# Modulation vectors as plain float32 matmuls on four column groups, spread over the layer; the latent-attention rotation folded into the score product

## The reference, cut to what matters

```python
mod = jax.nn.silu(c) @ w_ada[l] + b_ada[l]          # c for latents, c_ctx for the prompt
shift1, scale1, gate1, shift2, scale2, gate2 = jnp.split(mod, 6, axis=-1)
h = rms_norm(x, norm1) * (1 + scale1) + shift1
x = x + gate1 * mixing(h)            # differential, latent (MLA) and windowed attention
h = rms_norm(x, norm2) * (1 + scale2) + shift2
x = x + gate2 * expert_choice_ffn(h) # 16 experts, top-k per expert
```

## Time and profile before

| | us |
|---|---|
| median of 3 runs | 3476.33 (3473.27 to 3481.16) |
| the profiled execution | 3475.3, span 3473.5, mean TensorE clock 0.953 |
| TensorE busy (matmuls) | 3142.9 (90%) |
| VectorE busy | 2289.6 (66%) |
| ScalarE busy | 1699.7 (49%) |
| modulation stage, first matmul to first value product, layer 0 / layer 1 | 89.85 / 90.36 |

### The profile page before, as it was taken

One profiled execution on the slowest core, in us unless ns is written; L12 is line 12 of the kernel. 1 busy time (PEld: TensorE's weight loads), 2 busy tenths in 40 slices (PEclk: granted clock), 3 DMA queues, 4 the chain that ended last, 5 costly groups with the idle time before them and its releaser, 6 DMA issues.

```text
span 3473.5 us, 44790 instructions
## 1 busy us (share of the span) xinstructions
PE 3142.9 (90%) x15742; PEld 2212.6 (64%) x15742; DVE 2289.6 (66%) x3210; ACT 1699.7 (49%) x2471; POOL 0.2 (0%) x4
## 2 busy tenths in 40 slices
PE   6988998999978999999889889889899699999994
PEld 2466765667646777777636567557676477777773
DVE  6446535566548888888772654456653688888884
ACT  4425133224126777777573523331420477777773
POOL 0000000000000000000000000000000000000000
PEclk9999999999989999999899999999999799999996
DMA  8410110020217888888781001000112298888881
GB/s 298 178 55 1 60 50 1 26 87 1 103 49 257 303 296 315 314 306 314 243 316 63 31 33 52 26 25 26 63 37 91 89 322 308 308 315 313 314 313 45
DMA packets 276469, 551.00 MB, mean 159 GB/s; under 512 B 13608, under 2 KB 19424, under 8 KB 275680
## 3 DMA queue, kind: packets, MB, share of 16 engines
q1 hardware_dynamic: 273024, 543.32, 43.9%
q10 hardware_dynamic: 3296, 5.67, 0.5%
HBM read 537.52 MB, written 11.44 MB: 158 GB/s over the span
## 4 chain that ended last, share of the span: by engine, by line
PE 77%; DVE 9%; ACT 7%; issue 3%; DVEq 2%; ACTq 2%; DMA 0%; SPq 0%
PE mm L1281 26%; PE mm L791 14%; PE mm L749 11%; PE mm L793 4%; PE mm L853 3%; DVE w_lo L1814 2%; PE mm L821 2%; PE mm L1247 2%; PE mm L1029 2%; PE oo L1260 2%; PE oo L1049 1%; ACT scratch L1356 1%; ACTq L1750 1%; DVE tmp L1814 1%; PE mm L919 1%
## 5 line engine op out<-in xcount | busy, mean ns | idle before, releaser
L1814 DVE TENSOR_TENSOR w_lo<-ring,w_hi 128x1024 fp32r<-128x1024 f32 x864 | 1029.2, 1222 | 102.4 <-ACT w_hi L1356 82.6
L1356 ACT ACTIVATE w_hi<-ring 128x1024 fp32r<-128x1024 f32 x864 | 909.5, 1060 | 302.2 <-PE mm L1281 258.3
L1356 ACT ACTIVATE dw_hi<-ring 128x512 fp32r<-128x512 f32 (+1 forms) x168 | 104.4, 627 | 618.3 <-PE mm L793 612.9
L1814 DVE TENSOR_TENSOR dw_lo<-ring,dw_hi 128x512 fp32r<-128x512 f32 (+1 forms) x168 | 114.9, 689 | 366.1 <-ACT dw_hi L1356 365.6
L791 PE MATMUL mm<-h_hi,dw_lo 128*128 128x512 f32 (+1 forms) x672 | 327.0, 487 | 15.7 <-DVE dw_lo L1814 9.6
L793 PEld LDWEIGHTS mm<-h,ring 128*128 128x128 f32 (+1 forms) x1344 | 256.2, 191 | 61.2
L791 PE MATMUL mm<-h_hi,dw_hi 128*128 128x512 f32 (+1 forms) x672 | 269.5, 401 | 0.0
L791 PE MATMUL mm<-h_lo,dw_hi 128*128 128x512 f32 (+1 forms) x672 | 267.7, 398 | 0.0
L749 PE MATMUL mm<-scratch,ring 128*128 128x512 f32 (+3 forms) x896 | 260.2, 443 | 1.6 <-ACT scratch L1356 1.6
L793 PE MATMUL mm<-h,ring 128*128 128x128 f32 (+1 forms) x1344 | 260.5, 276 | 0.0
L749 PEld LDWEIGHTS mm<-scratch,ring 128*128 128x128 f32 (+1 forms) x896 | 141.3, 191 | 115.3 <-issue 112.9
(11 more groups left out here) (259 smaller groups left out, 5067.7 us busy)
## 6 DMA issues: line engine op xcount, KB each, us to landing
ring<-in_w_ff SPq DMA_DIRECT2D x384, 1024.0 KB, 6.0
ring<-in_w_ada SPq DMA_DIRECT2D x48, 1024.0 KB, 5.5
ring<-in_w_gate SPq DMA_DIRECT2D x24, 1024.0 KB, 6.6
ring<-in_w_in SPq DMA_DIRECT2D x16, 1024.0 KB, 10.0
ring<-in_w_o SPq DMA_DIRECT2D x8, 1024.0 KB, 7.5
x_spill<-x SPq DMA_DIRECT2D x2, 2560.0 KB, 10.6
ring<-in_w_br_da SPq DMA_DIRECT2D x4, 1024.0 KB, 6.8
ring<-in_w_br_mla SPq DMA_DIRECT2D x4, 1024.0 KB, 6.2
```

The source lines that it names most:

```text
L1356: return act.activation(out, in_, ACT.Copy, scale=scale)
L1814: return dve.tensor_tensor(out, in0, in1, op)
```

## The change

**Modulation.** The products are plain float32, without the hi/lo split. A block of 512 columns is 8 matmuls: the k-th 128 channels' part of the vector (2 columns, padded with zeros to 32) against ring tile k; tiles 0 to 3 write to PSUM rows 0, 32, 64 and 96 (four column groups of the array), tiles 4 to 7 add to them. ScalarE copies all 128 rows out, and small matmuls with a 0/1 matrix `fold` sum the four groups and turn the row to columns.

**Where it stands.** Blocks 0 to 3 (shift1, scale1) are first in layer 0; blocks 4 to 6 stand behind the differential attention, 7 to 9 behind the MLA heads, 10 and 11 behind the transposes of `h` in the router, and there in layer 0 also layer 1's blocks 0 to 3. So layer 1 begins with its norm at once. The spill of `x` is issued by ScalarE as soon as `x` is ready.

**MLA.** The query product has 128 output rows: 64, the 32 rotary ones, and the 32 swapped ones, whose weights GpSimd writes into the ring slot. VectorE takes them out of PSUM with two instructions, the second multiplying with a table of cos and sin (`turn32`); the key's rotary rows are there twice, so the score over 128 rows sums both parts. ScalarE now copies all transposed probabilities, ahead of the exponent.

The diff, cut to its core:

```diff
+ADA_BLOCKS = {"ada_first": range(4), "ada_x": range(4, 7), "ada_y": range(7, 10), "ada_z": range(10, 12)}
...
     for b in (2, 0, 1):
         block("in", b * BR)
+    modulation("ada_x")
     gates(0, "br_da")
     block("in", MLA_AT, QR + KVR + MROPE)
     block("in", SWQ_AT)
     out.append(("qb", 0, 0, MH * MQ))
     out.append(("kvb", 0, 0, MH * (MNOPE + MV)))
+    modulation("ada_y")
     gates(1, "br_mla")
     block("in", SWK_AT, 2 * SW_KV * DH)
     gates(2, "br_swa")
     for b in range(2):
         block("o", b * 512)
+    modulation("ada_z")
     return out
     FIRST.setdefault(_c[0], _i)
...
+    ("ada_first", 4), ("norm1", 1), ("da_v", TT), ("da_q", 4), ("da_k_rot", 12), ("da_s", 2), ("ada_x", 3),
     ("da_out", 16), ("mla_in", 10), ("kr_rot", 1), ("mla_v", KEY_TILES),
-    ("mla_heads", MLA_N + 3 * MH), ("mla_out", 16), ("sw_kv_rot", 7),
-    ("sw_s", 2), ("sw_out", 16), ("o", 8), ("norm2", 1), ("router", 1), ("gather_p", 2),
+    ("mla_heads", MLA_N + 2 * MH), ("ada_y", 3), ("mla_out", 16), ("sw_kv_rot", 7),
+    ("sw_s", 2), ("sw_out", 16), ("o", 8), ("norm2", 1), ("router", 1), ("ada_z", 2), ("ada_next", 4), ("gather_p", 2),
     ("pairs", 0)])
...
+                if kind in ADA_BLOCKS:
+                    return a["w_ada"][l, r0:r0 + HALF * P, c0:c0 + width].rearrange("(k p) c -> p k c", p=P)
...
+                def load_first(of, base):
+                    for n in range(FIRST_CHUNKS):
+                        g = base + n
+                        b, k0 = divmod(n, 2)
+                        sp.wait_ge(chunks_free, g + 1)
+                        sp.dma_start(ring[g % RING][:, :, :], chunk_source(of, "ada_first", k0 * HALF, b * 512, 512))\
+                            .then_inc(slot_in[g % RING], 16)
...
+                if l < DEPTH - 1:
+                    load_first(l + 1, PAIR_BASE[l] - FIRST_CHUNKS)
...
-                for n in range(24):
-                    pool.wait_ge(w_ready, ada_part(l, n * UNITS + UNITS - 1))
-                    pool.sem_inc(chunks_free, 1)
+                if l == 0:
+                    for b in range(4):
+                        consumed(MM["ada_first"] + b, 2)
                 consumed(MM["da_v"] + TT - 1, 2)
                 consumed(MM["da_q"] + 3, 2)
                 consumed(DA_K[3], 2)
+                for b in range(3):
+                    consumed(MM["ada_x"] + b, 2)
                 consumed(MM["da_out"] + 7, 3)
                 consumed(MM["da_out"] + 15, 3)
                 consumed(MM["mla_in"] + 3, 2)
                 consumed(SW_Q[3], 2)
+                pool.wait_ge(slot_in[slot(l, FIRST["qb"])], 16 * chunk_use(l, FIRST["qb"]))
+                pool.wait_ge(qb_in, l * 16 + 16)
+                w_ = ring[slot(l, FIRST["qb"])][:, :, :].rearrange("p k c -> p (k c)").rearrange("p (n c) -> p n c", c=P)
+                rot = w_[:, :, MNOPE:MQ].rearrange("p n (i two) -> p n i two", two=2)
+                swapped = w_[:, :, MQ:P].rearrange("p n (i two) -> p n i two", two=2)
+                pool.tensor_scalar(swapped[:, :, :, 0], rot[:, :, :, 1], -1.0, None, ALU.mult)
+                pool.tensor_copy(swapped[:, :, :, 1], rot[:, :, :, 0]).then_inc(wq_ready, 1)
                 consumed(mla_prep(MH - 1, 2), 2)
+                for b in range(3):
+                    consumed(MM["ada_y"] + b, 2)
...
+            def modulate(l, turn, base):
+
+                wait_mm_empty(pe, l, turn)
+                for half in range(2):
+                    g = base + half
+                    pe.wait_ge(slot_in[g % RING], 16 * (g // RING + 1))
+                    for kk in range(HALF):
+                        last = pe.matmul(mm[turn % 2][32 * kk:32 * kk + 32, 0:512], c_cols[:, half * HALF + kk, :],
+                                         ring[g % RING][:, kk, :], start=(half == 0), stop=(half == 1))
+                last.then_inc(mm_full[turn % 2], 1)
+
+            def fold_blocks(l, j, last_turn, blocks):
+
+                wait_mm_read(pe, l, last_turn)
+                if len(blocks) > 1:
+                    wait_mm_read(pe, l, last_turn - 1)
+                wait_t_empty(pe, l, j)
+                for n, row in enumerate(blocks):
+                    for m in range(4):
+                        last = pe.matmul(tp[:, 8 * n + 2 * m:8 * n + 2 * m + 2], row[:, m * P:(m + 1) * P], fold[:, :],
+                                         start=True, stop=True)
+                last.then_inc(t_full, 1)
...
+                if l == 0:
+                    pe.wait_ge(silu_ready, 1)
+                    for b in range(4):
+                        modulate(l, MM["ada_first"] + b, 2 * b)
+                    fold_blocks(l, TR["ada"], MM["ada_first"] + 3, [ada_row[1][:, b, :] for b in range(4)])
+                norm_of_x(l, MM["norm1"], l * 2 + 1)
...
+                for b in range(3):
+                    modulate(l, MM["ada_x"] + b, CHUNK_BASE[l] + FIRST["ada_x"] + 2 * b)
+                fold_blocks(l, TR["ada_x"], MM["ada_x"] + 2, [ada_row[0][:, b, :] for b in range(3)])
...
                     if piece == 0:
-                        product(mm[j % 2][0:MQ, :], lambda k: wqb[:, k, hd * MQ:(hd + 1) * MQ],
-                                lambda k: cq[:, k, :], 2).then_inc(mm_full[j % 2], 1)
-                    elif piece == 1:
+                        product(mm[j % 2], lambda k: wqb[:, k, hd, :], lambda k: cq[:, k, :], 2)\
+                            .then_inc(mm_full[j % 2], 1)
+                    else:
                         for lo, hi in ((0, 512), (512, KEYS)):
                             last = pe.matmul(mm[j % 2][0:MNOPE, lo:hi], wkvb[:, hd, 0:MNOPE], ckv[:, lo:hi],
                                              start=True, stop=True)
                         last.then_inc(mm_full[j % 2], 1)
-                    else:
-                        pe.sem_inc(pe_waited, 1)
-                        pe.matmul(mm[j % 2][MNOPE:MQ, 0:NLAT], c_("swap32", slice(MNOPE, MQ)),
-                                  ml_q[hd % 2][MNOPE:MQ, 0:NLAT], start=True, stop=True).then_inc(mm_full[j % 2], 1)
                 pe.wait_ge(kr_ready, l + 1)
                 pe.transpose(tp[:, 0:P], ckv[:, T:KEYS], ident)
                 pe.transpose(tp[:, P:P + MROPE], ml_k[0][MNOPE:MQ, T:KEYS],
                              ident[MNOPE:MQ, MNOPE:MQ]).then_inc(t_full, 1)
...
+                for b in range(3):
+                    modulate(l, MM["ada_y"] + b, CHUNK_BASE[l] + FIRST["ada_y"] + 2 * b)
+                fold_blocks(l, TR["ada_y"], MM["ada_y"] + 2, [ada_row[0][:, b, :] for b in range(3)])
...
+                z_blocks = 2 if l == DEPTH - 1 else 6
+                for b in range(z_blocks):
+                    modulate(l, MM["ada_z"] + b, CHUNK_BASE[l] + FIRST["ada_z"] + 2 * b)
+                fold_blocks(l, TR["ada_z"], MM["ada_z"] + z_blocks - 1, [ada_row[1][:, b, :] for b in range(z_blocks)])
...
+                def rows_in(turn, row):
+                    wait_mm_full(act, l, turn)
+                    copy(row, mm[turn % 2][:, 0:512]).then_inc(mm_empty[turn % 2], 1)
+
+                act.wait_ge(x_ready, l * 2 + 1)
+                act.dma_start(a["x_spill"], x[:, :, :]).then_inc(x_spilled, 16)
+                squares_of_x(l, 0, 0, lambda k: None)
+                if l == 0:
+                    for b in range(4):
+                        rows_in(MM["ada_first"] + b, ada_row[1][:, b, :])
+                first_rstd(l, 0)
                 shifts(l, 0, 0)
...
                 for s in range(MLA_N + 2):
+                    if s >= 2:
+                        mla_copy(s - 2)
                     if s < MLA_N:
                         hd, t = divmod(s, TT)
-                        if 1 <= t <= 2 and hd < MH - 1:
-                            head_in(hd + 1, t - 1)
+                        if t == 2 and hd < MH - 1:
+                            keys_in(hd + 1)
                         mla_exp(s)
-                    if s >= 2 and s % 2 == 0:
-                        mla_copy(s - 2)
                 wait_o_full(act, l, OO["mla"] + MLA_U - 1)
                 hi_of_tile(l, H_AT["mla_gate"])
+                for b in range(3):
+                    rows_in(MM["ada_y"] + b, ada_row[0][:, b, :])
                 gates(l, MM["mla_out"], lambda: None, H_AT["mla_gate"])
...
+                for b in range(2 if l == DEPTH - 1 else 6):
+                    rows_in(MM["ada_z"] + b, ada_row[1][:, b, :])
...
+                def modulation_in(j, at, n, bias):
+                    wait_t_full(dve, l, j)
+                    return tt(mod[:, at:at + n, :], tp[:, 0:2 * n].rearrange("p (m g) -> p m g", g=2),
+                              bias.unsqueeze(2).to_broadcast([P, n, 2]), ALU.add)
+
+                def gains(n, name):
                     lo, hi = ROWS[name]
                     for g in range(2):
                         stt(gain[:, n, :, g], mod[:, 24 * n + 8:24 * n + 16, g], 1.0, cols[:, lo:hi],
                             ALU.add, ALU.mult)
+
+                b0 = ROWS["b_ada"][0]
```

(32 more changed lines are left out.)

304 lines of the change are left out of this document (128 added, 176 removed).

## The result

| | before | after |
|---|---|---|
| median | 3478.74 us (4 runs, 3473.27 to 3481.27) | 3394.39 us (4 runs, 3392.12 to 3397.75) |
| ratio | | 0.976, 95% interval 0.9743 to 0.9777 |
| span of the profiled execution | 3473.5 | 3392.0 |
| TensorE busy, mean clock | 3142.9, 0.953 | 3054.5, 0.949 |

Forecast were 3393 us and a gain of 83; measured were 3394.4, and 81.5 between the two profiled spans. The total is nearer than its terms were, by luck: misses in both directions cancelled. This table goes through both traces at the same landmarks, the changed kernel less the one before; its last column is the sum of the two layers against the forecast's.

A forecast was written before the change was run, and what follows sets the result against it. TensorE's lines were the largest in the chain of waits; arithmetic and loads both bound modulation. Terms -59.5 - 74 - 34 + 13 + 34 + 34.5 + 3 = -83 took 3475.3 to 3392, or 3393 as median; range 3355 to 3435.

The forecast's parts named there:

- Price of a block: Modulation block's eight matmuls: four column groups run side by side, 1.7 us at the high clock level, 3.4 at the low.
- Front of layer 0: Layer 0's start to the first value product: 59.5 us less, values at 66.2 instead of 125.7, bounds 60 and 72.
- A fold costs as the old transposes: Fold after modulation blocks: 0.065 us a record, two records per matmul, 2.1 us for 16 matmuls, double at the low level.
- Front of layer 1: Layer 1's start, with no block left there: 74 us less, values at 1751 instead of 1825.2, bounds 1747 and 1757.
- Blocks 4 to 6: Behind the differential attention: 6.5 us more a layer, gate chunks being issued only when block 0 is done; bounds 4 and 12.
- It starts the gate tile at 317.1: Behind the differential attention: TensorE starts the gate tile at 317.1, against 310.7, and waits inside it for the second half.
- Blocks 7 to 9: Behind the MLA heads: 17 us more a layer, block 2's PSUM bank being freed only behind the gate chunks' rounding; bounds 10 and 24.
- Routers: Blocks 10, 11 and layer 1's four: 29 us more in layer 0 (bounds 20 and 45), 5.5 in layer 1 (3 and 10).
- Heads: MLA heads: 17 us less a layer from the dropped swap product and fewer waits of the transposes; bounds 3 and 25.
- A head takes 17.7 us: MLA heads before the change: time of one head read from the trace, 572.12 - 554.42 = 17.7 us.
- the item-by-item reckoning: MLA heads: instructions followed through both orders, starting when engine and inputs are there; a head 18.3 us before, 16.4 now.
- Arithmetic and loads both bind it: Old modulation stage: TensorE busy 73.9 of 83.7 us, loads 82 us at 306 GB/s, so cheaper blocks alone win nothing.

The follow-up runs named there:

- norm_first: Changed kernel, but in layer 0 the first norm's product and vector work stand ahead of the fold of the modulation rows; 3386.32 us, 0.9739 of the kernel before.
- Late_wait: Changed kernel, but TensorE waits for the branch's own chunk behind the first gate tile (and the fifth), not ahead; 3390.82 us, 0.9755 of the kernel before.
- Rows_first: Changed kernel, but ScalarE copies the three modulation rows behind the MLA heads before rounding the gate chunks; 3388.17 us, 0.9741 of the kernel before.
- own_layer: Changed kernel, but layer 1's first four blocks stand at layer 1's start, not in layer 0's router; 3379.61 us, 0.9731 of the kernel before.

## Why the prediction was right, point by point

- **Price of a block.** Right: 1.7 us at the high level.
- **Front of layer 0.** The step that failed is "A fold costs as the old transposes", 0.065 us a record and double at the low level. It is 0.12 (2.84 / 24) and 0.22 (6.99 / 32). The records differ in the stationary side: the fold's is a full 128 x 128 block, the old transposes' was two rows, and the weight load alone takes 0.19 us (0.33 at the low level) where the old one took 0.14. The fold was 7.0 us there for 2.1, the last chunk 2 us early, and 55.3 came out of 59.5; norm_first shows that the fold counted in full.
- **Front of layer 1.** Right: -73.4 for -74.
- **Blocks 4 to 6.** Inside the bounds (4 to 12), but 10.6 a layer for 6.5. The step "It starts the gate tile at 317.1" let the tile start on the first chunk; the code waits for three. I had read the order of instructions and not what one wait covers. Late_wait shows it.
- **Blocks 7 to 9.** Right in mechanism and size, 17.3 and 18.4 for 17. Rows_first confirms the bank as the link. The fold there was taken at 2.5 us (662.2 to 664.7), where its own price, doubled for the low level, is 3.1; it measured 3.35.
- **Routers.** 31.8 and 6.7 for 29 and 5.5: the fold was 7 us more, the loads 5 us faster. Right as a price, but the forecast never asked what the same blocks would cost where they came from; own_layer shows that this part of the change is a loss of some 15 us.
- **Heads.** 22 a layer for 17 less 1.5. "A head takes 17.7 us" was one pair of rows; over six of layer 0's heads the spacing is (609.51 - 500.46) / 6 = 18.2, which the item-by-item reckoning had as 18.3, and I took the trace's single pair for its fault. The 16.4 of the new head was 16.18. GpSimd's swap cost 0.8 us for 1.5.
- **The clock.** Left out of the sum. In the windowed stages it gave 5.4 us. In the heads it is an estimate of some 5 us a layer, what the swap product leaves of the busy time that went (13.3 us in layer 0, 11.3 in layer 1); no run took it apart.
- **What bound the old modulation stage.** "Arithmetic and loads both bind it" took 306 GB/s for what the loads can do. It is a mean that holds pauses of the loads: 358 GB/s while they ran without one, 0.01 share in the 4 us from 68.5. So the chunks' spacing of 3.4 us, used in the front and the router, was too long, and the loads were early there by 2 and 5 us.

So the total was right within 1.5 us by luck, because 20.7 us of costs missed (fronts 4.8, attention 2.0, blocks 8.2 and 1.7, routers 4.0) stood against 19.2 of gains missed (heads 12.9, windowed 5.4, the rest 0.9). Each term that had bounds stayed within them.

## What to carry to other kernels

Price a moved piece at both ends: what it costs in the new place and what it cost in the old with everything that ran beside it; here a start of a layer, with 8 us of vector work and a load to wait for, was cheaper than the router. Before a tile is said to start "when its chunk lands", read what its wait covers, since one wait for three chunks lasts as long as the last. And a chain of vector and scalar work (here a norm) gains by standing ahead of independent TensorE work of the same length (7.4 us in norm_first). A rate taken from a stage's mean holds the stage's pauses; for a forecast of loads alone, take it from a window in which they do not pause.

## What the runs showed of the hardware

- Four column groups ran four float32 passes in the time of one, 0.43 us for 512 columns.
- A matmul with two columns and a 128 x 128 float32 block as its stationary side costs 0.12 us a record high and 0.22 low; with two rows as its stationary side it was 0.065 high (3.10 / 48).
- The same 721 matmul records took 100.3 to 105.2 us in different kernels, at a granted clock of 0.97 and 0.92 at the two ends, with nothing edited in this stretch. Gains under 5 us are therefore read in their own stretch.
- Six modulation chunks of 1.05 MB landed every 2.7 us in the router, 389 GB/s. The modulation stage before had 306 on its mean, with pauses, 358 in the 20 us from 40, and 388 in the 3.1 us from 119.5. What makes the difference between the last two stays open.
- A higher clock went with fewer gaps: 0.95 to 1.00 in the heads, and folds of 3.7 to 3.9 us for 7.0 where TensorE had been busy just before.
